# A two-layer neighbourhood-attention kernel: the bias added by TensorE, one maximum per head, exponentials from the bank

## The reference, cut to what matters

```python
def row_block(args):
    q_row, r, r0 = args
    ...
    s_loc = jnp.einsum('bqhd,brkhd->bhqrk', q_row, k_band).astype(jnp.float32) * ATTN_SCALE
    row_off = r0 + jnp.arange(kr) - r + NA_ROWS_MAX - 1
    bias = rpb[:, row_off][:, :, col_bias_idx].transpose(0, 2, 1, 3)
    s_loc = jnp.where(col_in[None, None, :, None, :], s_loc + bias[None].astype(jnp.float32), -jnp.inf)
    s_ctx = jnp.einsum('bqhd,bkhd->bhqk', q_row, k_c).astype(jnp.float32) * ATTN_SCALE
    s_all = jnp.concatenate([s_loc.reshape(B, NA_HEADS, GRID_W, n_loc), s_ctx], axis=-1)
    prob = jax.nn.softmax(s_all, axis=-1).astype(v_band.dtype)
    ...
    o = (jnp.einsum('bhqrk,brkhd->bqhd', p_loc, v_band)
         + jnp.einsum('bhqk,bkhd->bqhd', prob[..., n_loc:], v_c))
```

## Time and profile before

| what | value |
|---|---|
| median of three runs | 2662.97 us |
| the profiled execution's own time | 2657.36 us |
| its span, first to last instruction | 2655.6 us |
| TensorE busy, share of the span | 2527.4 us, 95% |
| VectorE, ScalarE, GpSimd busy | 64%, 47%, 7% |
| mean granted TensorE clock | 0.982 |
| first score product of the second layer's attention | 889.64 us |
| first product of its output projection | 948.37 us |

### The profile page before, as it was taken

One profiled execution on the slowest core, in us unless ns is written; L12 is line 12 of the kernel. 1 busy time (PEld: TensorE's weight loads), 2 busy tenths in 40 slices (PEclk: granted clock), 3 DMA queues, 4 the chain that ended last, 5 costly groups with the idle time before them and its releaser, 6 DMA issues.

```text
span 2655.6 us, 41751 instructions
## 1 busy us (share of the span) xinstructions
PE 2527.4 (95%) x16957; PEld 2234.3 (84%) x16957; DVE 1702.6 (64%) x3153; ACT 1235.3 (47%) x2227; POOL 190.1 (7%) x235
## 2 busy tenths in 40 slices
PE   6999989999989999999999999999999999999998
PEld 3666568888867689999989979899899899798997
DVE  4664845455576566677657677776766577677764
ACT  3443733323255554454445455544544445555443
POOL 1000000000034210000000012000000000120001
PEclk8999999999999999999999999999999999999998
DMA  7655722233326335456555425465765544253654
GB/s 255 203 187 180 233 79 96 96 97 96 106 78 127 85 98 166 169 165 180 162 167 155 155 75 175 127 191 163 202 187 166 162 154 149 76 172 120 191 163 123
DMA packets 504159, 393.74 MB, mean 148 GB/s; under 512 B 26152, under 2 KB 472880, under 8 KB 503968
## 3 DMA queue, kind: packets, MB, share of 16 engines
q1 hardware_dynamic: 501168, 384.92, 47.7%
q0 software_dynamic: 2080, 3.53, 1.1%
q10 hardware_dynamic: 720, 2.62, 0.3%
HBM read 389.99 MB, written 1.05 MB: 147 GB/s over the span
## 4 chain that ended last, share of the span: by engine, by line
PE 85%; DVE 9%; ACT 2%; issue 1%; DMA 1%; POOL 1%; SPq 0%; DVEq 0%; ACTq 0%
PE pv L797 34%; PE pa L797 31%; PE pv L1245 6%; PE pv L762 4%; PE pa L762 4%; PE pv L1244 3%; DVE Wl L2014 3%; PE pa L767 2%; PE pa L951 1%; ACT Wh L1502 1%; DMA ring<-in_w_mod_dram 1%; DVE HTl L2021 0%; DVE TMP L2105 0%; POOL BIG L2730 0%; DVE HTl L2112 0%
## 5 line engine op out<-in xcount | busy, mean ns | idle before, releaser
L2014 DVE TENSOR_TENSOR Wl<-ring,Wh 128x1024 fp32r<-128x1024 f32 (+4 forms) x688 | 758.2, 1143 | 266.7 <-ACT Wh L1502 263.2
L1502 ACT ACTIVATE Wh<-ring 128x1024 fp32r<-128x1024 f32 (+4 forms) x688 | 641.0, 979 | 496.1 <-PE pv L797 330.3
L797 PE MATMUL pa<-HTl,Wh 128*128 128x256 f32 (+1 forms) x1648 | 535.5, 325 | 37.1 <-DVE HTl L2112 23.3
L797 PE MATMUL pv<-HTl,Wh 128*128 128x256 f32 (+1 forms) x1872 | 540.3, 289 | 15.9 <-DVE T L2448 5.8
L797 PE MATMUL pv<-HTh,Wl 128*128 128x256 f32 (+1 forms) x1872 | 538.6, 288 | 0.0
L797 PE MATMUL pv<-HTh,Wh 128*128 128x256 f32 (+1 forms) x1872 | 538.6, 288 | 0.0
L797 PE MATMUL pa<-HTh,Wl 128*128 128x256 f32 (+1 forms) x1648 | 518.7, 315 | 0.0
L797 PE MATMUL pa<-HTh,Wh 128*128 128x256 f32 (+1 forms) x1648 | 518.2, 314 | 0.0
L797 PEld LDWEIGHTS pv<-HTl,Wh 128*128 128x128 f32 x1872 | 360.8, 193 | 21.7 <-issue 12.6
L797 PEld LDWEIGHTS pa<-HTl,Wh 128*128 128x128 f32 x1648 | 317.1, 192 | 70.3 <-issue 43.6
L797 PEld LDWEIGHTS pv<-HTh,Wh 128*128 128x128 f32 x1872 | 360.8, 193 | 2.7
(11 more groups left out here) (266 smaller groups left out, 3247.3 us busy)
## 6 DMA issues: line engine op xcount, KB each, us to landing
ring<-in_ffn_w_gu_dram SPq DMA_DIRECT2D x176, 512.0 KB, 5.1
ring<-in_w_mlp_dram SPq DMA_DIRECT2D x64, 1024.0 KB, 5.2
ring<-in_w_mod_dram SPq DMA_DIRECT2D x48, 1024.0 KB, 5.7
ring<-in_ffn_w_down_dram SPq DMA_DIRECT2D x64, 704.0 KB, 4.5
ring<-in_w_in_dram SPq DMA_DIRECT2D x42, 1024.0 KB, 5.2
ring<-in_a_w_qkv_dram SPq DMA_DIRECT2D x12, 1024.0 KB, 5.2
ring<-in_b_w_qkv_dram SPq DMA_DIRECT2D x12, 1024.0 KB, 5.1
ring<-in_w_out_dram SPq DMA_DIRECT2D x8, 1024.0 KB, 5.3
```

Source lines behind the costliest of these rows:

```text
L797: m = nc.tensor.matmul(o, lhsT=x, rhs=y, start=first and j == 0, stop=last and j == 2)
L1502: ins = nc.scalar.activation(Wh[rows, p % SPLIT, a:b], ring[rows, i % RING, a:b], ACT.Copy)
L2014: ins = v.tensor_tensor(Wl[rows, p % SPLIT, a:b], ring[rows, i % RING, a:b], Wh[rows, p % SPLIT, a:b].bitcast(F32), ALU.subtract)
```

## The change: what it does

- TensorE issues three products for each head instead of one: the identity (128 by 128) times the bias tile into the latent half of the bank, the scores of the latent keys added onto it, and the scores of the context keys into the other half.
- The wait for the masked bias moves from VectorE's list to TensorE's.
- VectorE takes one maximum for each head over the 512 columns of the bank and negates it; `Lb` is not written.
- ScalarE takes the exponentials from the bank, and this frees the bank (before, VectorE's second reduce did).
- The outputs go to the last two A banks in turn, with `o_full` and `o_free`, and the transposes have the first two A banks (before, four). V holds scores alone.

```diff
--- before.py
+++ after.py
@@ -478,6 +478,8 @@
         A, V = Pool(pa, a_full, a_free), Pool(pv, v_full, v_free)
         mod_sum = pa[BANKS - 1]
         O_BANK = pa[BANKS - 2]
+        NEAR_O = pa[BANKS - 2:]
+        FIRST_O = 4 * DA_HEADS
 
         w_ready = [sem(f"w_ready{i}") for i in range(RING)]
         w_used = sem("w_used")
@@ -1083,14 +1085,21 @@
 
             def near_attention(tag):
 
+                A.width = 2
                 for s in range(len(NEAR_STEPS) + 3):
                     if s < len(NEAR_STEPS):
                         pair, t = NEAR_STEPS[s]
+                        if pair % 2 == 0 and t == 0:
+                            pe.wait_ge(bias_ok, seen.more(bias_ok, 8))
                         for m in range(2):
+                            h = 2 * pair + m
                             if V.taken():
                                 pe.wait_ge(v_free, V.taken())
-                            mm(V.take((tag, "S", s, m))[:, 0:512], Qn[sub(m), pair, t * P:(t + 1) * P],
-                               Ka[sub(m), pair, 0:512], True, True, v_full)
+                            b = V.take((tag, "S", s, m))
+                            mm(b[:, LAT], C("ident"), bias[h // 4][:, t, h % 4, :], True, False)
+                            mm(b[:, LAT], Qn[sub(m), pair, t * P:(t + 1) * P], Ka[sub(m), pair, LAT], False, True)
+                            mm(b[:, CTX], Qn[sub(m), pair, t * P:(t + 1) * P], Ka[sub(m), pair, CTX], True, True, v_full)
+                            V.emptied_otherwise((tag, "S", s, m))
                     if 0 <= s - 2 < len(NEAR_STEPS):
                         for m in range(2):
                             ready = pn_ready if m else dv_ready
@@ -1104,15 +1113,15 @@
                     if s >= 3:
                         pair, t = NEAR_STEPS[s - 3]
                         pe.wait_ge(a_free, A.nth((tag, "T", s - 3, 1)))
-                        if V.taken():
-                            pe.wait_ge(v_free, V.taken())
-                        b = V.take((tag, "O", s - 3))
+                        if s >= 5:
+                            pe.wait_ge(o_free, FIRST_O + s - 4)
+                        b = NEAR_O[(s - 3) % 2]
                         for k in range(4):
                             for m in range(2):
                                 h = 2 * pair + m
                                 mm(b[sub(m), 0:P], Va[:, k, h * HEAD:(h + 1) * HEAD],
                                    near_pt(s - 3)[:, m, k * P:(k + 1) * P], k == 0, k == 3,
-                                   v_full if k == 3 and m else None)
+                                   o_full if k == 3 and m else None)
 
             def first_layer(i):
                 if i == 0:
@@ -1184,7 +1193,8 @@
                     for pool, key in value_tiles(i, 1)[-2:]:
                         pe.wait_ge(pool.free, pool.nth(key))
                     near_attention(("att", i))
-                    pe.wait_ge(v_free, V.nth((("att", i), "O", len(NEAR_STEPS) - 1)))
+                    pe.wait_ge(o_free, FIRST_O + len(NEAR_STEPS))
+                    A.width = BANKS
                     N, tc = S, LAT
                     src = quarters(lambda k: O_AT["near"] + k)
                 for n in range(4):
@@ -1653,10 +1663,10 @@
                 for s in range(len(NEAR_STEPS) + 2):
                     if s < len(NEAR_STEPS):
                         for m in range(2):
-                            act.wait_ge(v_free, V.nth((tag, "S", s, m)))
-                            nc.scalar.activation(Pb[:, s % 3 * 2 + m, :], Lb[:, s % 2 * 2 + m, :], ACT.Exp,
-                                                 bias=nm[:, s % 2, m:m + 1], scale=-1.0,
-                                                 accum_out=rs[:, s % 3, m:m + 1]).then_inc(p_ready, 1)
+                            act.wait_ge(mx_ready, FIRST_O + 2 * s + m + 1)
+                            nc.scalar.activation(Pb[:, s % 3 * 2 + m, :], V.taken_at((tag, "S", s, m))[:, 0:512], ACT.Exp,
+                                                 bias=nm[:, s % 2, m:m + 1], scale=1.0,
+                                                 accum_out=rs[:, s % 3, m:m + 1]).then_inc(v_free, 1)
                     if s >= 2:
                         for m in range(2):
                             copy((tag, "T", s - 2, m), near_pt(s - 2)[:, m, :], lambda b: b[:, 0:512])
@@ -2240,20 +2250,12 @@
                 for s in range(len(NEAR_STEPS) + 3):
                     if s < len(NEAR_STEPS):
                         pair, t = NEAR_STEPS[s]
-                        if pair % 2 == 0 and t == 0:
-                            dve.wait_ge(bias_ok, seen.more(bias_ok, 8))
                         for m in range(2):
-                            h = 2 * pair + m
-                            key = (tag, "S", s, m)
-                            at, first = s % 2 * 2 + m, mx[:, s % 2, m:m + 1]
-                            dve.wait_ge(v_full, V.nth(key))
-                            b = V.bank(key)
-                            step(v.tensor_tensor_reduce(Lb[:, at, CTX], b[:, CTX], zeros(S), -1.0, -NEG,
-                                                        ALU.add, ALU.min, first))
-                            v.tensor_tensor_reduce(Lb[:, at, LAT], b[:, LAT], bias[h // 4][:, t, h % 4, :], -1.0, first,
-                                                   ALU.add, ALU.min, nm[:, s % 2, m:m + 1]).then_inc(v_free, 1)
+                            dve.wait_ge(v_full, V.nth((tag, "S", s, m)))
+                            v.tensor_reduce(nm[:, s % 2, m:m + 1], V.taken_at((tag, "S", s, m))[:, 0:512], axis=AXIS.X,
+                                            op=ALU.max, negate=True).then_inc(mx_ready, 1)
                     if 0 <= s - 1 < len(NEAR_STEPS):
-                        dve.wait_ge(p_ready, seen.more(p_ready, 2))
+                        dve.wait_ge(v_free, V.nth((tag, "S", s - 1, 1)))
                         u = (s - 1) % 3
                         v.reciprocal(rr[:, u, :], rs[:, u, :]).then_inc(rr_ready, 1)
                         dve.wait_ge(rr_ready, seen.more(rr_ready))
@@ -2261,8 +2263,11 @@
                     if s >= 3:
                         pair, t = NEAR_STEPS[s - 3]
                         j = O_AT["near"] + pair
-                        copy_in((tag, "O", s - 3), quarter(HTh, j)[:, t * P:(t + 1) * P],
-                                lambda b: backward(b[:, 0:P]), quarter(HTl, j)[:, t * P:(t + 1) * P])
+                        hi, lo = [quarter(x, j)[:, t * P:(t + 1) * P] for x in (HTh, HTl)]
+                        dve.wait_ge(o_full, FIRST_O + s - 2)
+                        o = backward(NEAR_O[(s - 3) % 2][:, 0:P])
+                        step(v.tensor_copy(hi, o))
+                        v.tensor_tensor(lo, o, hi.bitcast(F32), ALU.subtract).then_inc(o_free, 1)
 
             def two_heads(at):
 
@@ -2709,7 +2714,7 @@
                         pool.wait_ge(bias_late[c], 16 * 16)
                     for n in range(2 * part, 2 * part + 2):
                         mask_columns(2 + c, n)
-            pool.wait_ge(v_free, V.nth((("att", 1), "O", len(NEAR_STEPS) - 1)))
+            pool.wait_ge(o_free, FIRST_O + len(NEAR_STEPS))
             pool.dma_start(posi[:, :], spread(I["positions_2"], [[1, S]])).then_inc(pos_in, 16)
             pool.dma_start(memtok[:, :, :], I["mem_2"][0].rearrange("(t p) d -> p t d", p=P)).then_inc(mem_in, 16)
```

## The result

The changed kernel takes 2691.41 us, the median of four runs, against 2662.61, also of four; the ratio is 1.0111, interval 1.0098 to 1.0125. (One of its runs was disturbed, at 9769 us; it counts in the median, which without it is 2691.14, and not in the ratio.) The forecast was 2693.7. In the two profiled executions the span grew from 2655.6 to 2689.9, 34.3 us. The stage from the first score product to the first product of the output projection went from 58.73 us (889.64 to 948.37) to 89.66 (891.31 to 980.97), 30.9 us more.

The account below looks back on a forecast made before the run. TensorE sets the pace, busy 11.00 of 11.00 us at 3.11 us a step. Steps of 5.41 us and two mask stalls end the stage 30.7 us later: 2662.97 + 30.7 = 2693.7 us, range 2682 to 2700.

Parts of the forecast that it names:

- The heads apart: TensorE's scores: identity products keep the heads from running side by side; a step's scores take 3.37 us instead of 1.06.
- VectorE's relief: One plain maximum replaces two biased reduces per head: VectorE from 2.79 to about 2.4 us a step, worth 0 in steady state.
- the sum: Second layer's attention, added up from its first scores at 889.64 to the output projection at 979.1: stage ends 30.7 us later.
- the theory: Experiments' account of the longer step: heads no longer side by side 1.06 us, four identity records 0.86, two shape changes 0.4.
- Transpose banks, score banks, output banks: New bank waits cost 0: score banks have 5.8 us slack, transpose banks 2.6; outputs are copied one period before needed.
- The mask wait: Moved to TensorE: at steps 8 and 12 GpSimd's last masks take 6.54 us against a 5.41 period, stalling 1.13 us twice.
- Start and end: Three score-only steps of 3.366 us before the first transposes; last transposes to output projection 3.71 us, as now.
- The half-clock stretch: TensorE at 895 to 901, granted clock 0.50 before; should go to 1.00, since TensorE then has scores to do.
- 1 (changes of shape free): Changes of shape inside the score group cost nothing: period 4.83 us, time 2684; chance 0.13, including something between.
- 2 (identity products beside the scores): Identity products run beside the other head's scores: period 2.9 us, together -5.7 us, time 2657; chance 0.05.
- 3 (ScalarE's banks): ScalarE's chain binds through two transpose banks; each 0.5 us past its 2.6 slack adds 8 us, first 2702; chance 0.02.
- 4 (a new half-clock stretch): The two 1.13 us waits bring a half-clock stretch costing 3 us: 2697; counted within the forecast's 0.80.

Follow-up runs that it names:

- e2: Against the change: both heads' identity products first, then the split score products alternating between the heads; ratio 1.0057 to the kernel before.
- e3: Against the change: one whole 512-column score product for each head, then both identity products, next to the transposes; ratio 1.0051 to the kernel before.
- e4: Against the change: identity products left out, and with them bias and mask; the wait on TensorE stays; ratio 1.0019 to the kernel before.
- e5: Against e4: the wait for the mask also taken away from TensorE; ratio 0.9994 to the kernel before.
- e10: Against the kernel before: GpSimd masks the last two bias groups sooner, the last from step 7 on (three tiles, three, two); ratio 0.9997.
- e1: Against the change: both heads' identity products first, then head 0's two score products ahead of head 1's; ratio 1.0064 to the kernel before.
- e9: Against the change: each head has one 512-column score product, then its identity product, still head by head; ratio 1.0123 to the kernel before.
- e6: Against the change: GpSimd masks the last two bias groups sooner, each ready a step ahead of its first reader; ratio 1.0101 to the kernel before.
- e7: Against the kernel before: GpSimd masks the last two bias groups sooner, the last group from step 6 on; ratio 0.9998.

## Why the prediction was right

The 30.9 us, split by kernels that differ in one thing each (the last pair in several). "Start" is from the first score to the first transposes, "steps" from there to the last transposes; from the last transposes to the output projection it is 3.7 us in all of them.

| from, to | what goes | start, us | steps, us | stage, us |
|---|---|---|---|---|
| change, e2 | the heads apart, two changes of shape | 2.65 | 14.38 | 17.0 |
| e2, e3 | one change of shape | 0.06 | 2.70 | 2.8 |
| e3, e4 | the four identity records | 0.03 | 9.01 | 9.0 |
| e4, e5 | the mask wait on TensorE | 0.00 | 3.61 | 3.6 |
| e5, before | all the rest | 0.13 | -1.63 | -1.5 |

These are net figures, not prices. From the change to e2 the step falls by 1.25 us, 16.2 over the thirteen intervals with scores, and 1.8 of it comes back in longer waits (0.6 at each mask, 0.65 at the end). From e3 to e4 it falls by 0.91, 11.8 over thirteen; 2.0 comes back because e4 runs its first two intervals partly at half clock, and 0.9 in waits. The last row is mainly the price of VectorE's mask waits before, 0.79 us twice.

- **The bound.** TensorE set the pace and still does. VectorE's relief came (5.18 us busy in 11 instead of 9.88) and was worth nothing: e5 and e10, where neither has a mask wait, differ by 0.16 us. The relief was put a little too high: 5.18 in 11 is 2.55 us a step, not 2.4, and VectorE waits 2.0 us a step for scores, not more than 2.5. Nothing in the sum hangs on it.
- **Pieces from rows elsewhere.** Identity group 0.63, scores of a head 1.06, head 1.68, step 5.42 (5.41 predicted). The rows of other stages with the same rows, columns and neighbours gave the unseen mixture to 0.01 us.
- **The heads apart**, with the two changes of shape that it brings, was the largest term: 1.25 us a step (the change less e2), against 0.91 for the identity records (e3 less e4). That the overlap is what goes is shown by e1, e2 and e9; how the 1.25 divides is only reckoned: two changes at the 0.15 of e3 leave 0.95 for the overlap, where the theory has 1.06.
- **Transpose banks, score banks, output banks.** TensorE's products wait for none of them in the change, as predicted. The prediction had these slacks right only for the change as it stood: with shorter scores the third pair waits for the exponential (1.05 us in e3, 3.4 in e4), and the last transposes but one wait 0.5 to 0.8 us for ScalarE's copy in e1 to e5. Neither makes much of the stage: the start is 7.36 to 7.46 us in all five, 7.23 before.
- **The mask wait.** 1.08 us twice, 1.13 predicted; e6 takes back 2.3. The prediction read its price before as 0.6 us; with the interval after it (3.30) it is 0.79, which its sum, being added up from the start, did not use.
- **Start and end.** First transposes 10.10 us after the first score (10.10 predicted), last transposes to projection 3.70 (3.71). The half-clock stretch went.
- **The sum.** 30.9 measured for the stage, 30.7 predicted. The median's 28.8 differs from it by less than single runs of one kernel do (2655.75 to 2663.18 before).
- **Rivals.** 1 (changes of shape free) would have given a step of 4.83; 2 (identity products beside the scores) and 3 (ScalarE's banks) are refuted by the period and the absence of waits; 4 (a new half-clock stretch) did not occur, since the granted clock stays at 1.00 through both 1.08 us waits.

## What to carry to other kernels

Before moving work to the engine that sets the pace, find what already runs side by side on it. A full-array product put between two half-array ones costs their overlap: here 1.25 us a step with its changes of shape, where the product's own group is 0.63. Keep products of one shape together (all 64-row scores, then the full-array ones next to the transposes); if the change must stay, that alone takes back 20 of its 31 us.

A wait moved to the pacing engine holds up all that is queued behind it there: at the same step of 3.11 us the wait for the masks cost 0.79 us each on VectorE (before) and 1.74 on TensorE (e4). Its producer is to be moved forward with it, but not so far that it meets its own DMA, as in e7.

And do not take a wait's length for its price: in e4 one of 3.4 us stood where 2.02 had stood, and the work behind it came 0.13 us later. The start of the stage tells, not the wait.

## What the runs showed of the hardware

Two heads' score records overlap even when head 0's four are issued ahead of head 1's four: eight records in 1.07 us (e1), about the same as in alternation (1.06 to 1.07, e2). The expectation had left this open. And an fp32 product of 256 columns costs two records of 0.2155 us at full clock, 0.43 in all; e3 less e4 agrees: 0.91 us a step for two of them, of which 0.86 is records and 0.05 stays open.
